# Expert items in pairs: one fp32r gather for two items, and the scatter in fp32r passes

## Chip, core and metric

The kernel runs on one core of one Trainium2 chip. The metric is the device time in microseconds. The kernel before was run three times: median 2162.56 us, from 2161.83 to 2163.13.

## What is computed

The program takes one sequence of 256 tokens with 1024 features through two blocks. The first has two attention layers, the second two layers of a convolution and delta-rule mixer, each followed by a feed-forward part: dense in the first layer, a mixture of experts in the second. The change lies in that last part and in the layer norm behind it. All numbers are fp32.

```
def moe_swiglu(x, router_w, w_gate, w_up, w_down):
    logits = (x @ router_w).astype(jnp.float32)
    top_v, top_i = lax.top_k(logits, TOP_K)
    gates = jax.nn.softmax(top_v, axis=-1)
    combine = jnp.sum(jax.nn.one_hot(top_i, N_EXPERTS) * gates[..., None], axis=-2)
    y = jnp.zeros_like(x)
    for e in range(N_EXPERTS):
        y = y + combine[..., e:e + 1] * swiglu(x, w_gate[e], w_up[e], w_down[e])
    return y
...
x = layer_norm_2(DEEPNORM_ALPHA * x + f, ln_ffn_g[layer], ln_ffn_b[layer])
```

TOP_K is 2, N_EXPERTS 8 and D_FF_EXPERT 3584, so one expert has 3 x 1024 x 3584 weights, 44 MB.

## The kernel before

**Items.** The 256 tokens lie in two tiles of 128. Each expert takes its tokens in a block of up to 128, an *item*; an expert with more tokens gets a second item (`list_items`, L2662). The engines loop over the items with a count read from memory (`Fori`), and the last item stands behind the loop. For each item the kernel gathers the columns of its tokens out of x by a matmul with a 0/1 matrix `pick` (`gather`, L1449), computes the two hidden products and the down product, and adds the result to `total` through a second matmul with the transposed, weighted matrix `pickT` (`scatter`, L1470).

**Precision.** A fp32 matmul is done by TensorE in several passes. The large products use fp32r operands in three passes: every operand is split into a rounded high part and a low part, and high x high, high x low and low x high are summed in PSUM (L1485 to L1487, L1502). Weights are split on the chip: ACT copies a piece into `his` (`split_hi`), DVE subtracts (`split_lo`, L2626). The gathered x is split in the same way (`gathered_hi`, `gathered_lo`, L2702), and so are the hidden values (`hidden_hi`, `hidden_lo`, L2714). The gather and the scatter themselves are plain fp32.

**Pieces and turns.** The weights of an item are 42 pieces of 1 MB (`piece_of`), which SP loads into 14 slots; `his` has three buffers. The work on the pieces goes in turns (`chunk(n, j)`, j from 0 to 6, and -2 and -1 ahead of the loop). A turn takes six pieces: four for one 512 wide part of gate and up (`up_pieces`), two for the down product of the part before (`down_pieces`). Between them stands `turn_hidden` (L1464), which transposes the hidden values into bank 4; ACT makes `he_hi` out of it, DVE `he_lo`, and `down_pieces` waits for `he_ready`. In turn 5 the order differs: its two down pieces come first, they end the item, and the four up pieces belong to the next item. So turn 5 is where the next gather stands:

```
if j == 5:
    turn_hidden(g - 1)
    ...
    gather(0)
    pe.wait_ge(S("he_ready"), g)
    gather(1)
    down_pieces(n, g - 1, s0)
```

`turn_picks` (L1457) transposes the weighted picks in turn 0. In turn 6 PE waits for `ye_copied` and scatters three quarters into banks 5, 0 and 1 and the last into bank 5 again; DVE adds them to `total` (`add_out`, L2722).

**Order on the engines.** Each engine works through its own list in order, and the orders are written out by hand: in every turn ACT does `split_hi` of its six pieces with the other steps tied to a place r between them, and DVE the same with `split_lo`. In turn 5 DVE does `hidden_lo` behind the second split (r = 1), in the other turns behind the fourth. ACT may split piece s only when PE has used piece s - 3. SP loads piece s + 14 when PE has used piece s.

**Start and end.** At the start PE computes the logits (L1549), DVE finds the two best experts, the places and the first picks (L2640 to L2656), PE gathers, and DVE does `combine` and `list_items`; only then does SP know which expert to load from piece 14 on. At the end come the last hidden values, two down pieces, the copy of ye, four scatters, four adds, the statistics and the norm of each tile, and one store of x. SP loads the norm's rows `lng` and `lnb` ahead of the stage.

## Time and profile before

| | us |
|---|---|
| median of 3 runs | 2162.56 |
| the profiled execution | 2165.7 |
| its span, first to last instruction | 2163.9 |
| expert stage, from the first piece's matmul (1145.61) to the end | 1018 |
| one item, steady | 125.2 |
| granted clock of TensorE, mean over the span | 0.973 |

Below, a row of the timeline gives the start in us from the span's start, the duration, the engine and the line; names of tiles stand without buffer numbers. In brackets stands how long the engine was idle before it and what it waited for. A fp32 matmul leaves two records. Matmuls are pipelined, so a record's duration is longer than the distance to the next. The granted clock is 1.00 at 2.4 GHz and 0.50 at 1.2 GHz.

### The profile page before, as it was taken

The numbers are of one execution on the slowest core, as the hardware profiler recorded it, in microseconds if no ns is written. First come the engines' busy times: TensorE is split into PE (matmuls) and PEld (weight loads), VectorE is DVE, ScalarE is ACT, GpSimd is POOL, SyncE is SP. The second block draws the span as 40 slices with busy tenths as digits, with TensorE's granted clock in tenths as the row PEclk, the third lists the DMA queues.
The fourth block names the chain that finished last, engine by engine and source line by source line (L and its number), as shares of the span: only waits on it lengthen the run. The fifth ranks groups of instructions, "written<-read, shape, count | busy, mean of one in ns | idle before, by whom it ended". The sixth has DMA issues, their size and how long they took to land.

```text
span 2163.9 us, 27922 instructions
## 1 busy us (share of the span) xinstructions
PE 2097.1 (97%) x10564; PEld 1664.2 (77%) x10564; DVE 1505.0 (70%) x1822; ACT 1004.5 (46%) x1074; POOL 51.2 (2%) x56
## 2 busy tenths in 40 slices
PE   7999999999998999999889999999999999999996
PEld 4786577766876799888748888888888888888885
DVE  4465434554597544449848988888888888888886
ACT  1121312022233343313236767766776776777674
POOL 0000000000011000001200000000000000000000
PEclk9998999999999999999989999999999999999998
DMA  9844042610621355453127999999998999999890
GB/s 356 282 141 151 30 156 88 225 60 24 218 74 40 117 191 180 175 179 115 41 108 295 395 349 370 347 349 367 329 375 323 373 347 349 347 350 376 322 348 20
DMA packets 238695, 502.20 MB, mean 232 GB/s; under 512 B 11259, under 2 KB 53011, under 8 KB 238611
## 3 DMA queue, kind: packets, MB, share of 16 engines
q1 hardware_dynamic: 238610, 501.03, 64.4%
q8 instruction: 58, 0.95, 0.2%
q14 instruction: 27, 0.21, 0.0%
HBM read 499.96 MB, written 1.05 MB: 232 GB/s over the span
## 4 chain that ended last, share of the span: by engine, by line
PE 89%; DVE 7%; ACT 2%; issue 1%; DMA 0%; SPq 0%; DVEq 0%; ACTq 0%
PE bank L1502 12%; PE bank L1485 9%; PE bank L1487 9%; PE bank L1486 9%; PE bank L756 6%; PE bank L1195 6%; PE bank L1063 3%; PE bank L988 3%; PE bank L764 3%; PE bank L1165 3%; PE bank L1432 2%; PE bank L1171 2%; PE bank L1403 2%; PE bank L1402 2%; PE bank L1401 2%; PE bank L1367 2%
## 5 line engine op out<-in xcount | busy, mean ns | idle before, releaser
L2626 DVE TENSOR_TENSOR ring_r<-ring,his 128x2048 fp32r<-128x2048 f32 x240 | 549.2, 2291 | 83.3 <-ACT his L1598 83.2
L1598 ACT ACTIVATE his<-ring 128x2048 fp32r<-128x2048 f32 x240 | 460.4, 1919 | 130.9 <-PE bank L1487 77.6
L1485 PE MATMUL bank<-his,xe_hi 128*128 128x512 f32 x896 | 356.0, 397 | 0.2 <-DVE ring_r L2626 0.2
L1487 PE MATMUL bank<-his,xe_lo 128*128 128x512 f32 x896 | 349.5, 390 | 0.0
L1486 PE MATMUL bank<-ring_r,xe_hi 128*128 128x512 f32 x704 | 274.0, 389 | 0.0
L2626 DVE TENSOR_TENSOR more_raw_r<-more_raw,his 128x2048 fp32r<-128x2048 f32 x96 | 219.8, 2291 | 32.1 <-ACT his L1598 32.0
L1598 ACT ACTIVATE his<-more_raw 128x2048 fp32r<-128x2048 f32 x96 | 184.2, 1919 | 57.4 <-PE bank L1502 31.9
L1485 PEld LDWEIGHTS bank<-his,xe_hi 128*128 128x128 f32 x896 | 168.3, 188 | 36.1 <-issue 1.7
L1487 PEld LDWEIGHTS bank<-his,xe_lo 128*128 128x128 f32 x896 | 168.2, 188 | 35.8
L1486 PEld LDWEIGHTS bank<-ring_r,xe_hi 128*128 128x128 f32 x704 | 132.3, 188 | 28.3 <-issue 1.7
L1195 PE MATMUL bank<-uT,ring 128*128 128x256 f32 (+1 forms) x768 | 149.2, 356 | 0.0
L756 PE MATMUL bank<-uT,ring 128*128 128x256 f32 (+4 forms) x688 | 145.6, 368 | 0.0
L1502 PE MATMUL bank<-his,he_hi 128*128 128x512 f32 x448 | 142.5, 399 | 1.9 <-DVE he_lo L2714 1.9
L1195 PEld LDWEIGHTS bank<-uT,ring 128*128 128x128 f32 x768 | 130.6, 198 | 15.3 <-issue 0.5
L1502 PE MATMUL bank<-his,he_lo 128*128 128x512 f32 x448 | 138.5, 390 | 0.0
L756 PEld LDWEIGHTS bank<-uT,ring 128*128 128x128 f32 (+3 forms) x688 | 114.4, 184 | 27.4 <-issue 6.5
L2450 DVE SCALAR_TENSOR_TENSOR cacc<-hpad,cvec,cacc 128x256 f32<-128x256 f32 x240 | 109.7, 530 | 0.1
L1401 PE MATMUL bank<-uT_r,ff_hi 128*128 128x256 f32 (+1 forms) x384 | 108.6, 283 | 0.0
L2124 DVE TENSOR_TENSOR ring_r<-ring,ff_hi 128x2048 fp32r<-128x2048 f32 (+1 forms) x34 | 74.2, 2226 | 49.4 <-ACT ff_hi L1598 49.4
L1402 PE MATMUL bank<-u_lo,ff_hi 128*128 128x256 f32 (+1 forms) x384 | 108.1, 282 | 0.0
L1403 PE MATMUL bank<-uT_r,ring_r 128*128 128x256 f32 (+1 forms) x384 | 108.1, 282 | 0.0
L1598 ACT ACTIVATE ff_hi<-ring 128x2048 fp32r<-128x2048 f32 (+1 forms) x34 | 61.4, 1858 | 85.1 <-PE bank L1403 57.0
(427 smaller groups left out, 3076.2 us busy)
## 6 DMA issues: line engine op xcount, KB each, us to landing
ring<-in_moe_w_gate_dram SPq DMA_DIRECT2D x96, 1024.0 KB, 5.2
ring<-in_moe_w_up_dram SPq DMA_DIRECT2D x80, 1024.0 KB, 5.3
ring<-in_moe_w_down_dram SPq DMA_DIRECT2D x64, 1024.0 KB, 4.9
more_raw<-in_moe_w_down_dram SPq DMA_DIRECT2D x48, 1024.0 KB, 5.0
ring<-in_w_in_dram SPq DMA_DIRECT2D x16, 2048.0 KB, 10.9
more_raw<-in_moe_w_up_dram SPq DMA_DIRECT2D x32, 1024.0 KB, 5.2
ring<-in_w_ada_dram SPq DMA_DIRECT2D x12, 2048.0 KB, 10.4
ring<-in_w_out_dram SPq DMA_DIRECT2D x8, 2048.0 KB, 8.4
```

Source lines behind the costliest of these rows:

```text
L756: last = mm(b[0:n, to + tokens.start:to + tokens.stop], w[:, k, a:a + n], uT[:, k, tokens], start=(k == 0), stop=(k == KD - 1))
L1195: last = mm(b[:, f * T + tokens.start:f * T + tokens.stop], w[:, k, a:a + P], uT[:, k, tokens], start=(k == 0), stop=(k == KD - 1))
L1401: mm(o, hi[:, k, a], u_hi[:, k, tokens], start=(k == 0), stop=False)
L1402: mm(o, hi[:, k, a], u_lo[:, k, tokens], start=False, stop=False)
L1403: last = mm(o, lo[:, k, a], u_hi[:, k, tokens], start=False, stop=(k == KD - 1))
L1485: mm(bank[b][:, :], xe_hi[:, k, :], hi[:, kk, :], start=(k == 0), stop=False)
L1486: mm(bank[b][:, :], xe_hi[:, k, :], lo[:, kk, :], start=False, stop=False)
L1487: last = mm(bank[b][:, :], xe_lo[:, k, :], hi[:, kk, :], start=False, stop=(k == KD - 1))
L1502: last = mm(bank[6 + c][:, :], a[:, k, :], w[:, kk, 512 * c:512 * c + 512], start=(q == 0 and k == 0 and a is he_hi and w is hi), stop=(q ...
L1598: return go(out, in_, ACT.Copy, scale=scale)
L2450: ins = stt(cacc[:, f, :], src, w, cacc[:, f, :], ALU.mult, ALU.add)
L2626: tt(piece_lo(s), piece_raw(s), piece_hi(s).bitcast(fp32), ALU.subtract).then_inc(S("lo_ready"), 1)
```

## The change

Items are worked on in pairs. The loop body holds two items (a = 0 and a = 1), and the last pair stands behind the loop.

- **Gather.** x is split once into `x_hi` and `x_lo` (`x_lo` in the place of x, `xe_lo` in the place of `lng` and `lnb`, `x_hi` and `ye_lo` over constants no longer needed). `pick` is 256 columns wide, and one gather serves both items: 16 fp32r matmuls of 256 columns with `x_hi`, 16 with `x_lo`. Each of the four parts f is copied by ACT (high) and by DVE (low, now a plain copy). The gather stands in turn 5 of the second item only, spread between the pieces: part 0 ahead of the down pieces, 1 and 2 behind each of them, 3 between the first two up pieces.
- **Even items.** In turn 5 of the first item of a pair, `turn_hidden` is followed by `down_pieces` directly.
- **Scatter.** The picks are no longer weighted; `turn_picks` collects the weights of the slots into one column (`gslot`) by two fp32 matmuls of one column. ye is scaled with it and split: ACT writes `ye_hi`, DVE `ye_lo` (`out_lo`), and a scatter is two fp32r matmuls.
- **Start.** DVE computes `total` and `x_lo`, ACT `x_hi`, ahead of the logits; `combine` comes behind the splits of turn -2, and `list_items` is somewhat longer.
- **End.** The last down product goes by column halves (`last_down`), so do the copies and scatters; `hidden_lo` comes ahead of the last split; adds and statistics alternate; `lng` and `lnb` are loaded behind the last up piece; x is stored in two halves.

The constants' order in memory changes as well, with no work of its own. The diff, cut to its core:

```diff
+        const, const2 = sb("const", [P, NCONST]), sb("const2", [P, NCONST2])
+        x = sb("x", [P, NT, D])
+        lng, lnb = sb("lng", [P, D]), sb("lnb", [P, D])
...
+        x_hi = sb("x_hi", [P, NT, D], fp32r)
+        ye_lo = sb("ye_lo", [P, D], fp32r)
+        sb("const2_kept", [P, NCONST + NCONST2 - KEPT_FIRST - (NT + 1) * D])
+        x_lo = sb("x_lo", [P, NT, D], fp32r)
+        xe_lo = sb("xe_lo", [P, 2, KD, P], fp32r)
...
-                elif s == 2 * RING:
-                    norm_rows(sp, NORMS - 1, A["ln_ffn_g_2"][1], A["ln_ffn_b_2"][1])
...
+            sp.wait_ge(S("piece_used"), more * (2 * NPIECE) + (NPIECE + chunk_at(4) + 4))
+            norm_rows(sp, NORMS - 1, A["ln_ffn_g_2"][1], A["ln_ffn_b_2"][1])
+            for i in range(NT):
+                sp.wait_ge(S("x_ready"), NT * (NORMS - 1) + i + 1)
+                sp.dma_start(out_dram[0, i * P:(i + 1) * P, :], x[:, i, :]).then_inc(S("stored"), 16)
+            sp.wait_ge(S("stored"), 16 * NT)
...
+            def gather(m, f, lo, b):
+
+                if f:
+                    pe.wait_ge(S("xe_lo_ready" if lo else "xe_hi_ready"), m * 4 + f)
+                src = x_lo if lo else x_hi
+                for kk in range(2):
+                    k = 2 * f + kk
                     for i in range(NT):
+                        last = mm(bank[b][:, kk * 2 * P:(kk + 1) * 2 * P], src[:, i, k * P:(k + 1) * P], pick[:, i, :],
+                                  start=(i == 0), stop=(i == NT - 1))
...
+            def turn_picks(a):
+
+                own = slice(a * P, (a + 1) * P)
+                for i in range(NT):
+                    nc.tensor.transpose(bank[5][:, i * P:(i + 1) * P], pick[:, i, own].bitcast(fp32), C("ident"))
+                for i in range(NT):
+                    last = mm(bank[5][:, NT * P:NT * P + 1], pick[:, i, own].bitcast(fp32), combc[:, i, a:a + 1],
+                              start=(i == 0), stop=(i == NT - 1))
...
+                mm(bank[b][:, :], pickT[:, at // 2, :], ye_hi[:, cs], start=True, stop=False)
+                mm(bank[b][:, :], pickT[:, at // 2, :], ye_lo[:, cs], start=False, stop=True).then_inc(S("scattered"), 1)
...
+            def first_up(n, a, m, s0, b):
 
                 for half in range(2):
+                    if half:
+                        gather_both(m, 3)
+                    pe.wait_ge(S("xe_hi_ready"), m * 4 + (2 * half + 2))
+                    pe.wait_ge(S("xe_lo_ready"), m * 4 + (2 * half + 2))
+                    up_piece(n, a, s0 + half, half, b)
+
+            def gather_both(m, f):
+
+                gather(m, f, False, 5)
+                gather(m, f, True, 4)
...
+            def last_down(n, g, s0):
+
+                pe.wait_ge(S("he_ready"), g + 1)
+                for c in range(2):
+                    for half in range(2):
+                        s = s0 + half
+                        if c == 0:
+                            pe.wait_ge(S("lo_ready"), n * NPIECE + (s + 1))
+                        hi, lo = piece_hi(s), piece_lo(s)
+                        for kk in range(2):
+                            k = 2 * half + kk
+                            for a, w in ((he_hi, hi), (he_hi, lo), (he_lo, hi)):
                                 last = mm(bank[6 + c][:, :], a[:, k, :], w[:, kk, 512 * c:512 * c + 512],
+                                          start=False, stop=(k == 3 and a is he_lo))
+                    last.then_inc(S("last_down"), 1)
...
+                to = a if j < 5 else 1 - a
                 if j == 0:
                     pe.wait_ge(S("acc_added"), n * 4 + 4)
                 if j == 5:
                     turn_hidden(g - 1)
+                if j == 5 and a == 1:
                     pe.wait_ge(S("picks_copied"), n + 1)
-                    pe.wait_ge(S("picked"), n + 2)
-                    gather(0)
+                    pe.wait_ge(S("picked"), m + 2)
+                    gather(m + 1, 0, False, 5)
                     pe.wait_ge(S("he_ready"), g)
-                    gather(1)
+                    gather(m + 1, 0, True, 4)
+                    down_piece(n, s0)
+                    gather_both(m + 1, 1)
+                    down_piece(n, s0 + 1)
+                    gather_both(m + 1, 2)
+                    first_up(n, to, m + 1, s0 + 2, b)
+                    s0 += 2
+                elif j == 5:
                     down_pieces(n, g - 1, s0)
                     s0 += 2
-                if j == 5:
-                    pe.wait_ge(S("xe_ready"), n * 2 + 4)
-                up_pieces(n, s0, b)
+                    up_pieces(n, to, s0, b)
+                else:
+                    up_pieces(n, to, s0, b)
                 if j > -2 and j != 5:
                     turn_hidden(g - 1)
                 if j == 0:
...
+                    pe.wait_ge(S("ye_split"), n * 2 + 2)
+                    for at, bk in enumerate((5, 0, 1)):
+                        scatter(n, at, bk)
...
+                for f in range(4):
+                    gather(0, f, False, 5 + 2 * (f % 2))
+                    gather(0, f, True, 4 + 2 * (f % 2))
...
+                act.wait_ge(S("x_ready"), NT * (NORMS - 2) + 1)
+                copy(x_hi[:, 0, :], x[:, 0, :]).then_inc(S("x_hi_ready"), 1)
                 copy_tile(("moe", 0), 1, 1)
                 act.wait_ge(S("x_ready"), NT * (NORMS - 1))
+                copy(x_hi[:, 1, :], x[:, 1, :]).then_inc(S("x_hi_ready"), 1)
...
+                def gathered_hi(m, f, b):
+
+                    act.wait_ge(S("gathered_hi"), m * 4 + (f + 1))
+                    copy(xe_hi[:, :, 2 * f:2 * f + 2, :], bank[b][:, :].rearrange("p (k a s) -> p a k s", k=2, a=2))\
+                        .then_inc(S("xe_hi_ready"), 1)
...
                         if j == 5 and r == 4:
                             copy_out(n)
+                        if j == 5 and a == 1 and r in (1, 2, 3, 4):
+                            gathered_hi(m + 1, r - 1, 5)
...
+                j = jobs["moe", 0, "xT11"]
+                filled(dve, j)
+                for i in range(NT):
+                    for c in range(2):
+                        cs = slice(512 * c, 512 * c + 512)
+                        ts(total[:, i, cs], x[:, i, cs], ALPHA, None, ALU.mult).then_inc(S("acc_added"), 1)
+                for i in range(NT):
+                    dve.wait_ge(S("x_hi_ready"), i + 1)
+                    dve.wait_ge(S("acc_added"), 2 * i + 2)
+                    tt(x_lo[:, i, :], x[:, i, :], x_hi[:, i, :].bitcast(fp32), ALU.subtract).then_inc(S("x_lo_ready"), 1)
...
+                def gathered_lo(m, f, b):
+
+                    dve.wait_ge(S("gathered_lo"), m * 4 + (f + 1))
+                    nc.vector.tensor_copy(xe_lo[:, :, 2 * f:2 * f + 2, :], bank[b][:, :].rearrange("p (k a s) -> p a k s", k=2, a=2))\
+                        .then_inc(S("xe_lo_ready"), 1)
...
+                def out_lo(n):
+
+                    dve.wait_ge(S("picks_copied"), n + 1)
+                    for c in range(2):
+                        cs = slice(512 * c, 512 * c + 512)
+                        dve.wait_ge(S("ye_hi_ready"), n * 2 + (c + 1))
+                        stt(ye_lo[:, cs], bank[6 + c][:, :], gslot[:, 0:1], ye_hi[:, cs].bitcast(fp32), ALU.mult, ALU.subtract)\
+                            .then_inc(S("ye_split"), 1)
...
+                        if j == 5 and a == 1 and r in (1, 2, 3, 4):
+                            gathered_lo(m + 1, r - 1, 4)
...
+                        if j == 5 and r == 5:
+                            out_lo(n)
...
+                for f in range(4):
+                    gathered_lo(0, f, 4 + 2 * (f % 2))
+                chunk(0, 0, -2)
                 combine()
-                gathered_lo(0, [1])
-                chunk(0, -2)
                 list_items()
-                chunk(0, -1)
+                chunk(0, 0, -1)
...
                 gated(n, g, 4)
+                hidden_lo(g)
                 split_lo(n, s + 1)
-                hidden_lo(g)
-                for at in range(4):
-                    add_out(n, at, at)
-                dve.wait_ge(S("acc_added"), n * 4 + 8)
+                out_lo(n)
                 for i in range(NT):
                     for c in range(2):
+                        add_out(n, 2 * i + c, 2 * i + c, turn=NT * c + i)
+                        dve.wait_ge(S("acc_added"), n * 4 + (4 + 2 * i + c + 1))
                         half_stats(i, c, total[:, i, :])
                     norm(NORMS - 1, i, total[:, i, :])
 

```

## Rows read from the trace of the kernel before

**Rows 1.** The page's first part: busy us, share of the span and instructions of each engine.

```profile
PE 2097.1 (97%) x10564; PEld 1664.2 (77%) x10564; DVE 1505.0 (70%) x1822; ACT 1004.5 (46%) x1074; POOL 51.2 (2%) x56
```

**Rows 2.** By window: us, PE, PEld, DVE, ACT, POOL busy; clock, DMA share, GB/s.

```profile
1160.00:2134.00 974.00, 973.49 (x4460) 799.59 (x4461) 847.26 (x513) 697.90 (x475) 0.00 (x0) 1.00 0.94 346
1160.00:1180.00 20.00, 20.00 (x92) 16.25 (x93) 18.99 (x14) 14.36 (x9) 0.00 (x0) 1.00 1.04 399
```

**Rows 3.** The timeline of turn 5, first and seventh item: start, us, what.

```profile
1257.96 2.28 DVE L2626 TENSOR_TENSOR more_raw_r<-more_raw,his 128x2048 fp32r<-128x2048 f32 x1
...
1258.44 0.60 PE L1467 MATMUL bank<-const,uT 128*128 128x128 f32 x4
...
1258.87 4.08 PE L1453 MATMUL bank<-pick,x 128*128 128x128 f32 x32
...
1259.08 0.60 ACT L1598 ACTIVATE he_hi<-bank 128x512 fp32r<-128x512 f32 x1 [1.24 <-PE bank L1467]
...
1260.16 0.68 DVE L2714 TENSOR_TENSOR he_lo<-bank,he_hi 128x512 fp32r<-128x512 f32 x1
...
1262.70 0.70 PE L1502 MATMUL bank<-his,he_hi 128*128 128x512 f32 x2
...
1265.73 1.93 ACT L1598 ACTIVATE his<-ring 128x2048 fp32r<-128x2048 f32 x1 [0.34 <-PE bank L1502]
...
1270.29 0.39 PE L1485 MATMUL bank<-his,xe_hi 128*128 128x512 f32 x1
...
1270.97 0.39 PE L1485 MATMUL bank<-his,xe_hi 128*128 128x512 f32 x1
...
2011.41 0.69 DVE L2714 TENSOR_TENSOR he_lo<-bank,he_hi 128x512 fp32r<-128x512 f32 x1
```

**Rows 4.** The timeline of PE in the dense stage.

```profile
799.93 0.28 PE L1401 MATMUL bank<-uT_r,ff_hi 128*128 128x256 f32 x1
...
802.09 0.28 PE L1401 MATMUL bank<-uT_r,ff_hi 128*128 128x256 f32 x1
```

**Rows 5.** The timeline of PE at the last item's last hidden values.

```profile
2134.92 0.60 PE L1467 MATMUL bank<-const,uT 128*128 128x128 f32 x4
2137.45 1.07 PE L1502 MATMUL bank<-his,he_hi 128*128 128x512 f32 x2 [1.94 <-DVE he_lo L2714]
```

**Rows 6.** The timeline of PE at three scatters of the first item.

```profile
1285.01 2.74 PE L1472 MATMUL bank<-ye,pickT 128*128 128x512 f32 x6
```

**Rows 7.** The timeline of PE at matmuls of one column.

```profile
601.31 2.85 PE L1268 MATMUL bank<-const,sq 128*128 128x1 f32 x25
```

**Rows 8.** The timeline of DVE and PE at the start of the expert stage.

```profile
1132.42 2.29 DVE L2626 TENSOR_TENSOR ring_r<-ring,his 128x2048 fp32r<-128x2048 f32 x1 [2.11 <-ACT his L1598]
...
1139.90 5.95 PE L1453 MATMUL bank<-pick,x 128*128 128x128 f32 x32 [1.20 <-DVE pick L2656]
...
1154.61 2.29 DVE L2626 TENSOR_TENSOR ring_r<-ring,his 128x2048 fp32r<-128x2048 f32 x1
...
1170.31 1.43 DVE L2755 TENSOR_SCALAR total<-x 128x512 f32<-128x512 f32 x4
```

**Rows 9.** One line's instructions on DVE: duration min/median/max in ns, first and last start.

```profile
L2392 DVE TENSOR_TENSOR mix<-mix,sg x4: 1218/1222/1225, 252.6 to 497.7; 128x1024 f32<-128x1024 f32 x4
```

**Rows 10.** The timeline of PE and DVE at the end.

```profile
2145.94 3.70 PE L1472 MATMUL bank<-ye,pickT 128*128 128x512 f32 x8 [1.17 <-ACT ye L1598]
...
2158.16 1.28 DVE L2087 SCALAR_TENSOR_TENSOR x<-x,lnmv,lnb 128x1024 f32<-128x1024 f32 x1
```

**Rows 11.** Busy time and granted clock by window, behind three waits of PE.

```profile
643.00:646.00 3.00, 3.00 (x4) 1.33 (x5) 3.00 (x9) 0.00 (x0) 0.00 (x0) 0.50 0.00 0
1041.00:1044.00 3.00, 3.00 (x20) 2.28 (x20) 2.94 (x8) 0.60 (x1) 0.68 (x1) 1.00 0.00 0
2138.00:2141.00 3.00, 3.00 (x9) 2.32 (x8) 0.00 (x0) 0.00 (x0) 0.00 (x0) 0.50 0.00 0
```

**Rows 12.** The waits of PE: us in total, times, longest us.

```profile
PE bank L1207 <- DVE vb L2544: 5.3, 2, 2.7
```

More of the change, by code:

```diff
@@ L136, in constants @@
     later["level0"] = lv[:, 0].T.copy()
+    later["tri_le"] = (row <= col).astype(np.float32)
+    later["tri_lt"] = (row < col).astype(np.float32)
+    later["iota"] = np.broadcast_to(r[None, :], (P, P)).astype(np.float32)
+    parts["fill"] = np.zeros((P, -sum(v.shape[1] for v in parts.values()) % 64), np.float32)
     at = {}
@@ new lines, in _ @@
+            with sp.Fori(0, more) as m:
+                e = [sp.value_load(items[0:1, bass.ds(m * 2 + (2 * NE + after), 1)], min_val=0, max_val=NE - 1) for after in range(3)]
+                for s in range(RAWS, RAWS + 2 * NPIECE):
+                    sp.wait_ge(S("piece_used"), m * (2 * NPIECE) + (s - RAWS + 1))
+                    load_piece(s, bass.ds(e[piece_of(s)[1]], 1))
+            e = [sp.value_load(items[0:1, bass.ds(more * 2 + (2 * NE + after), 1)], min_val=0, max_val=NE - 1) for after in range(2)]
@@ new lines, in down_pieces @@
+                down_piece(n, s0 + 1)
[5 more added lines that the diff above has]
+                        if c == 0:
+                            pe.wait_ge(S("lo_ready"), n * NPIECE + (s + 1))
+                        hi, lo = piece_hi(s), piece_lo(s)
+                        for kk in range(2):
+                            k = 2 * half + kk
+                            for a, w in ((he_hi, hi), (he_hi, lo), (he_lo, hi)):
@@ L1538, in chunk, with first_chunk @@
                     down_pieces(n, g - 1, s0 + 4)
+            def first_chunk():
+                for half in range(2):
+                    pe.wait_ge(S("xe_hi_ready"), 2 * half + 2)
+                    pe.wait_ge(S("xe_lo_ready"), 2 * half + 2)
+                    up_piece(0, 0, half, half, 0)
+                up_pieces(0, 0, 2, 1)
             def experts():
@@ L2696, in gathered_lo @@
-                def gathered_lo(m, halves=(0, 1)):
-                    for half in halves:
-                        dve.wait_ge(S("xe_hi_ready"), m * 2 + (half + 1))
-                        b = bank[5 - half][:, :].rearrange("p (f s) -> p f s", f=4)
-                        hi, lo = xe_hi[:, 4 * half:4 * half + 4, :], xe_lo[:, 4 * half:4 * half + 4, :]
-                        tt(lo, b, hi.bitcast(fp32), ALU.subtract).then_inc(S("xe_ready"), 1)
+                    ts(comb[:, :, 2 * NE:], chosen[:, :, 0:1], 0.0, None, ALU.mult)
```

248 lines of the change are left out of this document (113 added, 135 removed).

## Prediction

> **What bounds the kernel now.** I read the page's busy times first: TensorE (PE) is busy for 97% of the span, DVE for 70%, ACT for 46% [rows 1]. The change lies in the expert stage, so the window over that stage comes next [rows 2]: from 1160 to 2134 PE is busy for 973.49 of 974 us at the full clock, DVE for 847, ACT for 698. PE bounds it. The weights are no bound: the window from 1160 to 1180 moved 399 GB/s, the whole stage 346 GB/s. One item loads 42 pieces of 1.049 MB, which at 399 GB/s is 110 us, while an item takes 125.2 us (DVE's he_lo of turn 5 starts at 1260.16 in the first item and at 2011.41 in the seventh, six items later) [rows 2, 3]. But DVE has only 13% idle, and PE is fed through three buffers: a piece is copied by ACT (1.92 us), subtracted by DVE (2.29 us), then multiplied in 12 matmuls 227 ns apart, 2.72 us (the starts at 1270.29 and 1270.97 are three matmuls apart) [rows 3]. What counts is therefore PE's own work per item, plus every wait that the new order of the instructions opens on PE.
>
> **The gather.** Before, an item's gather is 32 records (16 fp32 matmuls of 128 columns). With what it waits for it fills PE from 1258.87 to 1262.70, 3.83 us [rows 3]. A pair's gather is 32 fp32r matmuls of 256 columns. The dense stage has the same form: 18 of them from 799.93 to 802.09, 120 ns each [rows 4], so 3.84 us for a pair in place of 7.66.
>
> But the old gather also covers a chain. Turn 5 begins with four transposes of the hidden values (1258.44); ACT then writes he_hi, and DVE writes he_lo, but only after the split of piece 1 that stands ahead of it in DVE's order (1257.96 to 1260.24). he_lo ends at 1260.84 and the down matmuls may begin [rows 3]. PE fills that time with the gather.
>
> *Even items (four of them, 0, 2, 4, 6)* have no gather now: turn_hidden is followed at once by down_pieces, which waits for he_ready. The trace has exactly this case once, at the end of the last item: transposes at 2134.92, down matmuls at 2137.45, 2.53 us later [rows 5]. Before, that distance in turn 5 is 1262.70 - 1258.44 = 4.26 us. So an even item gains 1.73 us, not 3.83: 4 x -1.73 = -6.9 us.
>
> *Odd items with a gather (1, 3, 5).* PE does the transposes (0.43) and 4 matmuls (0.48), then waits for he_ready until about 2.5 us after the transposes began: a gap of 1.6 us. Later first_up's second half needs the last copy of xe_lo. Follow the chain from the end of gather 2's high part: 0.25 us until ACT sees it, ACT copies (0.60, as he_hi), ACT splits piece 4 (1.92), DVE splits it (2.29), and only then DVE copies the last low part (0.69), with 0.1 for the hand-overs: 5.85 us. PE has meanwhile gather 2 low (0.48), one piece (2.72) and gather 3 (0.96): 4.16 us. A second gap of 1.7 us. Turn 5 is then 0.43 + 72 x 0.227 + 3.84 + 1.6 + 1.7 = 23.9 us, against 20.7 before (0.43 + 3.83 + 16.4) [rows 3]: 3 x +3.2 = +9.6 us. The gathers of the loop together come to +2.7 us, where bare matmul time would give -15.3.
>
> **Scatter.** An fp32 matmul of 512 columns is two records. Six records last 2.74 us, each 0.59 and overlapping, so (2.74 - 0.59) / 5 = 0.43 us apart [rows 6]; four scatters take 8 x 0.43 = 3.44 us. Now 8 fp32r matmuls of 227 ns, 1.82 us: 7 x -1.62 = -11.3 us; the last item's is in the end. The split of ye moves to DVE (two operations of 0.69) ahead of turn 6's first split: ready at about 1279.13 where PE asks at 1279.13, so nothing. DVE's four adds cost 2.8 us in turn 6 against PE's 1.8 of scatter; by the rows' distances DVE then still comes 0.5 to 0.7 us before PE. I take 0, at most 0.5 per item (3.5 in all).
>
> **turn_picks.** The transposes stay; two fp32 matmuls of one column come, 4 records. The nearest row: 25 records of one column in 2.85 us, 114 ns each [rows 7]. 8 x 0.46 = +3.7 us. The Trainium skill (TensorE: Matmul & The Clock Gate, "Wait — 56ns, not 53.3ns?") says that start to start never falls under about 25 ns however few the columns; by that floor the term would be 0.8. The row carries a weight load with each matmul, as here, and it decides. The extra copy of gslot on ACT and the longer pick_tokens on DVE lie under PE.
>
> **The start.** DVE gets, ahead of the logits, four products of total (1.43 us; their old place cost PE nothing) and two subtractions of 128x1024 (1.22 us each in the nearest row) [rows 8, 9], and ACT two copies. The second x_lo ends at about 1133.6, the logits follow, and split_lo(0,0), which began at 1132.42, begins at 1134.1: +1.7 us. Two more picks: +0.5. The gather, at the low clock, was 5.95 us from 1139.90 on. The new one streams as many columns, but each part waits for the copy of the part before it; with the clock rising at the same distance I get 6.7. Piece 0 starts 3.0 us later. Then combine stands behind the splits of pieces 2 and 3 and list_items has some 0.8 us more: DVE's split of piece 4, which ended at 1156.90, ends at about 1162.1, PE waiting 2.6 us. Together +5.2 us. The loads of pieces 14 and on begin that much later too, with 20 us in hand. Between 3 and 8.
>
> **The end.** he_lo goes ahead of the last split, so the down matmuls begin 0.5 us sooner; the column halves hide half of the ye copies. The last scatter ends near 2146.6, where it ended at 2149.6 [rows 10]. DVE then mixes adds and statistics and finishes the last x at 2157.5, where it was 2159.4; and the last store is half as long: 0.9 us. -2.9 us, between -1.5 and -4. lng and lnb are loaded some 15 us ahead of their use.
>
> **Sum without the clock:** 2.7 - 11.3 + 3.7 + 5.2 - 2.9 = -2.6 us.
>
> **The clock.** After the wait at the end of the last item the granted clock is 0.50 (1.2 GHz) from 2138 to 2141 [rows 11]: three us do the work of 1.5, and with the ends of the stretch I count 1.7 us lost. The new gaps follow work as dense as that. But no gap of this size is sure to do it: line L1207 waits 2.7 us for vb once in each of the two mixers, and the first wait is followed by 0.50 (643 to 646), the second by 1.00 (1041 to 1044) [rows 11, 12]. So two gaps of three are followed by the low clock, and the new ones are mostly shorter than these: ten new gaps in the loop of 1.6 to 2.1 us and one of 2.6 at the start, a fall behind half or a little less; I take 5, +8.5 us (0 to 18.7).
>
> **Forecast:** +5.9 us. The profiled execution took 2165.7 us (span 2163.9), 3.1 over the median of 2162.56. On its scale 2171.6, on the median's 2168.5.
>
> **The rivals.**
> - *The gaps come, the clock stays up:* -2.6 us, 2160.0, no difference or nearly. For it: one gap of three left the clock alone, and the new ones are shorter than it. Against: the one gap behind turn_hidden in this very stage did not.
> - *The gaps don't come* (faster). It decides at he_ready and xe_lo_ready: if he_lo were written before the split of piece 1, or ACT and DVE ran a piece ahead, PE would find both ready. Then 4 x -3.83 for the even items, 0 for the odd: -15.3 - 11.3 + 3.7 + 5.2 - 2.9 = -20.6, 2142.0. For it: he_hi is ready by 1259.68, so only DVE's order makes the wait, and gather 1 is well spread. Against: all seven turns 5 have he_lo at the same place (a period of 125.2 us from the first to the last in [rows 3]), and DVE's order there is unchanged.
> - *More is lost:* every gap costs 1.7 us (+18.7): 2178.7. Or DVE, with 0.7 us more per item behind the scatter than PE gives it time for, stops PE in turn 0 as well: up to 3.5 us more.
> - *The pairs don't come out even:* an odd number of items would add an empty one, a whole item of 125 us. The period of 125.2 us goes seven times into the stage behind the first turn, so there are eight items and four full pairs; I give it nothing.
>
> **Chances.** Gaps with about half the falls 0.5 (2163 to 2174); gaps without falls 0.2; no gaps 0.12; more lost 0.15; 0.03 for anything else. A difference under 0.2% (4.3 us) a measurement can hardly tell. Slower by more: most of the first and all of the fourth, 0.55. Within: all but a little of the second, the low edge of the first, 0.27. Faster: 0.18. The range leaves out the case without gaps and the far end of the fourth: 2154 to 2178.
>
> **What would show it.** In turn 5 of even items, PE's waits for he_lo of about 2.0 us, four of them; in odd items one of 1.6 for he_lo and one of 1.7 for xe_lo; windows with a clock of 0.50 behind some; a scatter of 1.8 us; piece 4 of the first item about 5 us later; the last x at about 10 us after the last scatter. If PE's waits on DVE in the loop come to under 5 us instead of the 18 here, the step on he_ready is wrong and the kernel is faster. If they are there and no window of the loop has a clock under 1, the result is 2160.

## The result and the profile after

The changed kernel takes 2183.29 us (median of 4 runs, 2179.99 to 2188.47) where the kernel before takes 2162.36 (4 runs): a ratio of 1.0094, interval 1.0079 to 1.0109. It is 20.9 us slower; 5.9 were forecast. Every ratio below is to the kernel before, run beside it, with its 95% interval in brackets. The profiled execution took 2184.97 us with a span of 2183.2, 19.3 over the span of before.

The first part of the page answers to [rows 1]: TensorE (PE) is busy 7 us less, in a longer span. Below it the row of the queue that brings in instructions, which had 58 packets and 0.95 MB before.

```profile
PE 2089.9 (96%) x10468; PEld 1652.1 (76%) x10468; DVE 1514.0 (69%) x1841; ACT 1008.1 (46%) x1084; POOL 51.4 (2%) x56
...
q8 instruction: 90, 1.47, 0.3%
```

The waits of PE from 1150 us to the end, in us in total, times, longest. The kernel before has three there: 1.9 for he_lo, 1.2 for ye and 0.2 at piece 4.

```profile
PE bank L1532 <- DVE he_lo L2811: 7.6, 4, 1.9
PE bank L1501 <- issue: 5.7, 2, 3.1
PE bank L1499 <- DVE xe_lo L2798: 4.3, 3, 1.4
PE bank L1466 <- DVE he_lo L2811: 4.1, 3, 1.4
PE bank L1499 <- issue: 2.5, 2, 1.3
PE bank L1499 <- DVE ring_r L2722: 2.0, 1, 2.0
PE bank L1555 <- DVE he_lo L2811: 1.5, 1, 1.5
PE bank L1490 <- DVE ye_lo L2820: 0.6, 1, 0.6
PE bank L1555 <- DVE more_raw_r L2722: 0.5, 1, 0.5
```

The waits on DVE are those of the prediction. Not foreseen are the four called *issue*: PE's matmuls are late with nothing to wait for. The timeline shows them (start, us, what), together with turn 5 of an even item (1261.84, 1264.35), the scatter (1286.98), the two gaps of an odd item's turn 5 (1388.40, 1401.65), turn_picks' matmuls of one column (1439.50) and the end, which answers to [rows 3, 5, 6, 10].

```profile
1145.34 0.40 PE L1499 MATMUL bank<-his,xe_hi 128*128 128x512 f32 x1
...
1158.62 0.50 PE L1499 MATMUL bank<-his,xe_hi 128*128 128x512 f32 x1 [2.00 <-DVE ring_r L2722]
...
1261.84 0.60 PE L1484 MATMUL bank<-const,uT 128*128 128x128 f32 x4
1264.35 0.72 PE L1532 MATMUL bank<-his,he_hi 128*128 128x512 f32 x2 [1.91 <-DVE he_lo L2811]
...
1286.98 0.48 PE L1490 MATMUL bank<-ye_hi,pickT 128*128 128x512 f32 x1
...
1290.54 0.40 PE L1499 MATMUL bank<-his,xe_hi 128*128 128x512 f32 x1
...
1293.32 0.40 PE L1499 MATMUL bank<-his,xe_hi 128*128 128x512 f32 x1
...
1388.40 0.73 PE L1466 MATMUL bank<-pick,x_lo 128*128 128x256 f32 x4 [1.36 <-DVE he_lo L2811]
...
1401.65 0.49 PE L1499 MATMUL bank<-his,xe_hi 128*128 128x512 f32 x1 [1.43 <-DVE xe_lo L2798]
...
1430.37 0.49 PE L1499 MATMUL bank<-his,xe_hi 128*128 128x512 f32 x1 [1.18 <-issue]
...
1435.73 0.50 PE L1501 MATMUL bank<-his,xe_lo 128*128 128x512 f32 x1 [2.55 <-issue]
...
1439.50 0.51 PE L1476 MATMUL bank<-combc,pick 128*128 128x1 f32 x4
1439.86 0.47 PE L1499 MATMUL bank<-his,xe_hi 128*128 128x512 f32 x1
...
2159.89 0.49 PE L1555 MATMUL bank<-his,he_hi 128*128 128x512 f32 x1 [1.49 <-DVE he_lo L2811]
...
2167.97 0.50 PE L1490 MATMUL bank<-ye_hi,pickT 128*128 128x512 f32 x1 [0.64 <-DVE ye_lo L2820]
...
2178.80 1.28 DVE L2173 SCALAR_TENSOR_TENSOR x<-x,lnmv,lnb 128x1024 f32<-128x1024 f32 x1
```

1430.37 is the first matmul of the loop's second pass. The third pass begins with the same pair of stalls (1.30 and 3.13): 8.2 us in all, behind the loop's two jumps back. The kernel before jumps back six times and has none: its waits of PE over the same stretch name no *issue*.

The second thing not foreseen is in the distance of ordinary matmuls. From 1290.54 to 1293.32 lie 12 fp32r matmuls of 512 columns, 232 ns apart, where before it was 227 [rows 3]. Over the whole stage, three up matmuls take 0.6951 us on the mean (before 0.6817) and six down matmuls 1.3771 (before 1.3611). With 896 and 224 such groups that is 12.0 + 3.6 = 15.6 us.

The granted clock falls in two places of the loop only. By window: us, busy PE, PEld, DVE, ACT, POOL, clock, DMA share, GB/s.

```profile
1522.00:1525.00 3.00, 3.00 (x10) 2.34 (x10) 2.29 (x1) 0.28 (x1) 0.00 (x0) 0.64 0.72 277
1525.00:1528.00 3.00, 3.00 (x12) 2.40 (x11) 0.00 (x0) 1.67 (x1) 0.00 (x0) 0.79 0.23 23
...
1696.00:1699.00 3.00, 3.00 (x10) 2.40 (x9) 1.07 (x1) 1.90 (x1) 0.00 (x0) 0.66 0.55 153
```

The first follows a wait for he_lo, the second the issue stall of 3.13 us. The first costs 3 x 0.36 + 3 x 0.21 = 1.7 us, as a fall did in the prediction. The kernel before has a fall of its own, behind the wait of 1.94 us in the last item [rows 5, 11]; after, with 1.49 us there, has none: its clock is 1.00 from 2156 to 2165.

### The profile page after: what moved, and what is told of

Its sections match the earlier page's. It is cut to its first block, busy times and chain, and to the rows that moved or that the text cites. A ratio compares the mean times of both kernels' runs of the same rounds, so it can differ in the third digit from the quotient of the medians.

```text
span 2183.2 us, 27738 instructions
## 1 busy us (share of the span) xinstructions
PE 2089.9 (96%) x10468; PEld 1652.1 (76%) x10468; DVE 1514.0 (69%) x1841; ACT 1008.1 (46%) x1084; POOL 51.4 (2%) x56
## 4 chain that ended last, share of the span: by engine, by line
PE 88%; DVE 7%; issue 2%; ACT 2%; DMA 0%; SPq 0%; DVEq 0%; ACTq 0%
PE bank L1532 12%; PE bank L1501 9%; PE bank L1499 9%; PE bank L1500 9%; PE bank L765 6%; PE bank L1204 6%; PE bank L997 3%; PE bank L1072 3%; PE bank L773 3%; PE bank L1174 3%; PE bank L1441 3%; PE bank L1180 2%; PE bank L1410 2%; PE bank L1411 2%; PE bank L1412 2%
## 5 line engine op out<-in xcount | busy, mean ns | idle before, releaser
L1501 PE MATMUL bank<-his,xe_lo 128*128 128x512 f32 x896 | 355.1, 396 | 5.7 <-issue 5.7
L1532 PE MATMUL bank<-his,he_hi 128*128 128x512 f32 x440 | 136.8, 392 | 7.6 <-DVE he_lo L2811 7.6
L1532 PEld LDWEIGHTS bank<-his,he_hi 128*128 128x128 f32 x440 | 82.4, 189 | 26.2 <-DVE more_raw_r L2722 8.6
```

What stands on the lines that cost most here:

```text
L1501: last = mm(bank[b][:, :], xe_lo[:, a, k, :], hi[:, kk, :], start=False, stop=(k == KD - 1))
L1532: last = mm(bank[6 + c][:, :], a[:, k, :], w[:, kk, 512 * c:512 * c + 512], start=(q == 0 and k == 0 and a is he_hi and w is hi), stop=(q ...
```

## The experiments

Three theories had to be told apart. **Places:** the new buffers moved where the operands begin in SBUF, and that sets the matmuls' distance. **Layout:** the paired xe_hi and xe_lo (two items side by side) set it. **Loop:** the issue stalls come from the jump back to a longer body; the rival is that they come from the pairs' order of work. The table gives where each operand begins, as the remainder by 256 bytes of its start address in a partition (the *residue*; from the program's layout), and what the traces gave. *Streamed* operands are the pieces of the weights (his, ring_r, more_raw_r), *loaded* ones the stationary xe_hi, xe_lo and he. *Three up* is the distance from one high x high matmul to the next, three matmuls later; *six down* the same for the down product.

| kernel | ring_r | more_raw_r, his | xe_hi, he | xe_lo | three up, us | six down, us |
|---|---|---|---|---|---|---|
| before | 128 | 128 | 128 | 128 | 0.6817 | 1.3611 |
| after | 128 | 160 | 160 | 128 | 0.6951 | 1.3771 |
| e1 | 128 | 192 | 192 | 128 | 0.6965 | 1.3827 |
| e2 | 128 | 160 | 160 | 160 | 0.6916 | 1.3768 |
| e3 | 128 | 192 | 192 | 192 | 0.6877 | 1.3776 |
| e5 | 128 | 0 | 0 | 128 | 0.6933 | 1.3757 |
| e8 | 128 | 128 | 160 | 160 | 0.7001 | 1.3999 |
| e12 | 128 | 0 | 0 | 0 | 0.6911 | 1.3751 |
| e9 | 128 | 128 | 128 | 128 | 0.6820 | 1.3627 |
| e10 | 128 | 128 | 128 | 128 | 0.6818 | 1.3628 |
| e15 | 192 | 192 | 192 | 192 | 0.6819 | 1.3607 |

### Four first looks: e1 to e4

**e1**, the kernel after with everything behind `items` 32 bytes on:

```
         items = sb("items", [P, 4 * NE + 1], mybir.dt.int32)
+        sb("shift", [P, 8])
```

> The changed kernel with 32 unused bytes ahead of the staged tiles, so that his, more_raw, xe_hi and he_hi start on a multiple of 64 bytes again, as in the kernel before (in the changed kernel the longer constants moved them to an odd multiple of 32). Theory A, the start address sets the distance between the up matmuls: three of them take 0.681 us again instead of 0.695, 896 x 0.0136 = 12 us less than the changed kernel, some 2171. Rival B, the distance comes from the new shape or place of xe_hi and xe_lo, or from the longer loop: still 0.695 and no change, some 2183.

2184.38 us (4 runs), three up 0.6965: no gain. That a multiple of 64 is enough is refuted.

**e2**, the kernel before with the same line.

> The kernel before with the same 32 bytes, so that its staged tiles start on an odd multiple of 32 bytes. Theory A: three up matmuls take 0.695 us and the kernel is 12 us slower, some 2174.5. Rival B: 0.681 us and 2162.4, since neither shape nor place nor loop changed.

2176.3 us (4 runs), ratio 1.0060 (1.0042 to 1.0078), three up 0.6916, six down 1.3768. The kernel before, with not one instruction changed, lost 13 us by a shift of 32 bytes. Places matter by themselves.

**e3**, the kernel before with 32 bytes behind the constants and 32 ahead of the staged tiles, which moves x as the change does.

> The kernel before with 32 unused bytes behind the first constants and 32 ahead of the staged tiles: const2, x and the norm's rows move to a multiple of 64, the staged tiles stay on one. In the changed kernel the time up to the second tile's transposes ahead of the experts is 3.9 us shorter than before. Theory A: that comes from the address of x and const2, so the kernel is some 3.9 us faster, 2158.5, with those transposes near 1124. Rival: it is a matter of when the low clock falls and differs from run to run: 2162.4.

2168.93 us (10 runs), ratio 1.0024 (1.0015 to 1.0034), three up 0.6877. It is slower, not 3.9 us faster. Its one profiled execution, the fastest of the ten, does have the transposes early, at 1120.53, but so has that of e8 (1120.11), whose x kept its place. So the rival holds: that time differs between profiled executions, and nothing of it can be put down to the place of x.

The stage alone is free of that. From the first up matmul to the end of the span it takes 1018.3 us in before and in e15, 1024.7 in e3, 1027.3 in e12, 1028.2 in e2 and 1039.2 in e8: the order of the distances in the table. (Before and e15 each hold one clock fall under work, 1.7 us, in it, the other four none.)

**e4**, the kernel after with PE's loop over the pairs written out (the number of pairs fixed, as these inputs give it):

```
-                more = pe.value_load(...)
-                with pe.Fori(0, more) as m:
+                more = 3
+                for m in range(more):
                     for a in range(2):
```

> The changed kernel with TensorE's loop over the pairs written out three times (the number of pairs behind the loop is taken as three, as these inputs have it). In the changed kernel TensorE stands 1.2 and 2.6 us behind its first jump back and 1.3 and 3.1 behind its second, waiting for nothing that the profile names. Theory C, the jump back to a body twice as long costs them: the four gaps go, 8.2 us and a fall of the clock less, some 2173 to 2175. Rival D, the gaps come from something else at that place (loads of instructions as such): they stay, or others come all along the longer code, and the time stays near 2183 or rises.

2169.89 us (10 runs), 13.4 less than after. The stalls at the loop's start are gone. The trace still lists three of 1.29 under *issue* (1400.42, 1653.28, 1906.18): these are the three gaps for xe_lo, which carry another name there, since the 1.43 for xe_lo have gone from its list. So 8.2 us of stalls were taken away, the other gaps are 0.8 us shorter in all, and e4's profile has none of after's two clock falls (3.4 us). That is 12.4 us, where the medians differ by 13.4 and the two profiled spans by 14.4; the rest has no row.

### Multiples of 128, and the parts by themselves: e5 to e8

**e5**, the kernel after with 96 bytes ahead of the expert stage's staged tiles alone:

```
         place[0] = raws
+        sb("shift_raw", [P, 24])
...
         place[0] = fourth
+        sb("shift", [P, 24])
```

> The kernel after, with 96 bytes per partition put ahead of the expert stage's staged tiles alone, so that more_raw, his, xe_hi and he_hi begin at multiples of 128 bytes again as in the kernel before (xe_lo, at a multiple of 128 already, and x stay where they are). Theory A' (the matmuls' distance follows from where the tiles begin within 128 bytes; 32 and 64 bytes behind such a multiple both cost): three up matmuls back from 0.695 us to 0.682, six down matmuls from 1.377 to 1.361, and with 896 and 224 of them 12.0 + 3.6 = 15.6 us less, so about 2168. Rival B (the distance is a matter of the paired layout of xe_hi and xe_lo, 256 columns of two items, or of the rest of the changed program): 0.695 and 2183 as they were. Rival C (any move helps or harms by a couple of us): up triple between 0.685 and 0.69.

2180.37 us (5 runs), 0.6933 and 1.3757. 2168 was expected by the theory that a multiple of 128 is enough (A'). It falls, and the layout theory stands for the moment.

**e6**, the same with the loop written out.

> The same with TensorE's loop over the pairs written out three times, for the number of pairs that these inputs give. If the issue stalls come from the jump back and the distance from the places, the two add up: 13.4 us less for the loop as in the run that wrote it out alone, 15.6 less for the places: about 2183.3 - 29 = 2154, which would be below the kernel before (2162.4). If A' falls, about 2169 as the written-out kernel took before.

2169.01 us (8 runs), the case where A' falls.

**e7**, the kernel before with the scatter of the change alone:

```
-                mm(bank[b][:, :], pickT[:, at // 2, :], ye[:, ...], start=True, stop=True)
+                mm(bank[b][:, :], pickT[:, at // 2, :], ye_hi[:, cs], start=True, stop=False)
+                mm(bank[b][:, :], pickT[:, at // 2, :], ye_lo[:, cs], start=False, stop=True)
```

with turn_picks on unweighted picks, the weight as the copy's scale, and DVE's ye_lo as in the change.

> The kernel before with one part of the change alone: the scatter in two fp32r passes, with unweighted picks and the weight of each place as the scale of the copy. Per-item gather, the loop over items, the places of all staged tiles and the end over all columns stay. By the terms of the sum: seven items' scatters 7 x -1.62 = -11.3, turn_picks' two one-column matmuls 8 x 0.46 = +3.7, and at the end two more splits of 1.2 us ahead of the scatter and four shorter ones, about +0.5: 2162.4 - 7.1 = 2155.3. Rival: what TensorE gains is lost again in weaker cover (no gain, 2162), or the clock falls more often.

2153.64 us (6 runs), ratio 0.9958 (0.9942 to 0.9974): 8.5 us faster, 7.1 expected. Its staged tiles lie where they lay before, and the distance is 0.6823.

**e8**, the kernel before with 32 bytes between `his` and `xe_hi`.

> The kernel before with 32 bytes put between his and xe_hi: the moving operands (more_raw, his, ring) stay at multiples of 128 bytes, only the stationary ones (xe_hi, xe_lo, he_hi, he_lo) and what lies behind them move by 32. If the moving operand's place sets the distance: up triple 0.682, down six 1.361, time 2162.4. If the stationary one's does: 0.69 and 1.377, about 2176 as with all of them moved.

2182.97 us (5 runs), ratio 1.0098: the slowest distance of all. The timeline of PE; 12 matmuls take 2.80 us:

```profile
1201.58 0.40 PE L1486 MATMUL bank<-his,xe_hi 128*128 128x512 f32 x1
...
1204.38 0.40 PE L1486 MATMUL bank<-his,xe_hi 128*128 128x512 f32 x1
```

Here the streamed operands kept their place and only the loaded ones moved. It is neither kind by itself: compared with e2, where both moved by 32 bytes, it is worse. That points to how the two stand to each other.

The traces of e2, e3 and e12 show it within one kernel. There his, more_raw_r, xe_hi, xe_lo and he all agree, and only ring_r differs. A low piece lies either in more_raw_r or in ring_r. Three up matmuls with more_raw_r take 0.682 (e2), 0.683 (e3) and 0.684 us (e12), as in before; with ring_r they take 0.694, 0.689 and 0.693. In before both take 0.682 to 0.683, in e8 both 0.700. From e2's timeline, 12 matmuls with ring_r (2.77 us) and 12 with more_raw_r (2.72 us):

```profile
1283.79 0.39 PE L1486 MATMUL bank<-his,xe_hi 128*128 128x512 f32 x1
1284.02 0.40 PE L1487 MATMUL bank<-ring_r,xe_hi 128*128 128x512 f32 x1
...
1286.56 0.39 PE L1486 MATMUL bank<-his,xe_hi 128*128 128x512 f32 x1
...
1303.64 0.39 PE L1486 MATMUL bank<-his,xe_hi 128*128 128x512 f32 x1
1303.86 0.39 PE L1487 MATMUL bank<-more_raw_r,xe_hi 128*128 128x512 f32 x1
...
1306.36 0.39 PE L1486 MATMUL bank<-his,xe_hi 128*128 128x512 f32 x1
```

### The same residue of 256: e9 to e12, e15

**e9** and **e10** put 224 and 480 bytes where e5 put 96; e10 also has the loop written out.

> The kernel after with 224 bytes put ahead of the expert stage's staged tiles: more_raw, his, xe_hi and he_hi then begin 128 bytes behind a multiple of 256, as ring_r and xe_lo do and as all of them did in the kernel before. Theory A'' (what counts is that the operands, both the streamed and the loaded ones, begin at the same residue of 256 bytes): up triple 0.682 us, down six 1.361, 15.6 us less than 2183, about 2168. Rival B (the paired layout of xe_hi and xe_lo or the rest of the program sets the distance): 0.693 to 0.695, about 2181. The issue stalls behind the jump back stay either way.

> The kernel after with TensorE's loop over the pairs written out and 480 bytes put ahead of the staged tiles, so that each of them begins at the same residue of 512 bytes as in the kernel before. A'': 0.682 and 1.361 and 2169 - 15 = 2154. If 512 bytes are the period and not 256, only this one of the two gets 0.682. Rival B: 0.693 and 2169 for both.

e9 took 2174.15 us (7 runs, 2167.28 to 2177.3; the profiled span is 2168.0), e10 2160.77 (11 runs), ratio 0.9984 (0.9972 to 0.9996). Both have the distance of before (0.6820 and 0.6818), with the paired layout as it is. The layout theory falls. In e9's timeline 12 matmuls take 2.73 us:

```profile
1288.26 0.39 PE L1501 MATMUL bank<-his,xe_hi 128*128 128x512 f32 x1
...
1290.99 0.39 PE L1501 MATMUL bank<-his,xe_hi 128*128 128x512 f32 x1
```

Since 128 and 384 by 512 do equally well, the period is 256 bytes and not 512. e9 gained 9 us on the median (11 by the two ratios) where 15.6 were expected; on the profiled spans it is 15.2, 1.7 of them one clock fall less. Its distance is shown, its whole gain in time is not: the runs scatter over 10 us, and only one of them has a trace. e10 came out 6.8 us above the expectation; its profile has two clock falls, 3.4 us, and the other half has no row.

**e12**, the kernel before with 128 bytes ahead of the staged tiles.

> The kernel before with 128 bytes put ahead of the staged tiles: more_raw, his, xe_hi, xe_lo and he begin at multiples of 256 bytes, ring_r stays 128 bytes behind one. If multiples of 128 are enough (theory A', with the paired layout to blame for the rest): 0.682 and 1.361, 2162. If the operands need the same residue of 256 (A''): up triple about 0.69, six about 1.376, 2162 + 10 = 2172.

2172.39 us (11 runs, 2163.96 to 2177.29), ratio 1.0035 (1.0022 to 1.0048), three up 0.6911: as the theory of 256 bytes has it. That the median meets the expected 2172 to half a us is luck, with runs that far apart.

**e15**, the kernel before with 64 bytes ahead of everything, ring_r too.

> The kernel before with 64 bytes put ahead of everything, ring_r too, so that ring_r, more_raw_r, his, xe_hi, xe_lo and he all begin 192 bytes behind a multiple of 256 (128 in the kernel before). If only their agreement counts: up triple 0.682, six 1.361, 2162.4. If the residue 128 itself is what is fast (every fast layout so far had it): up triple 0.688 to 0.70, six about 1.377, 2170 or more.

2164.29 us (10 runs), ratio 1.0004 (0.9991 to 1.0017), 0.6819 and 1.3607. So no residue is special; the operands have to agree.

**e11**, e7 with the end of the change (last down pieces by column halves, adds and statistics by halves, a store for each tile).

> The kernel before with two parts of the change: the scatter in fp32r passes (2153.6 alone) and the end by column halves (the last down pieces by halves, last hidden_lo ahead of the last split, adds and statistics by halves, each x tile stored for itself). The term of the sum was -2.9, 0.5 of it the earlier hidden_lo: about 2150.7. Rival: the end gains nothing without the pairs, 2153.6.

2152.47 us (5 runs), ratio 0.9941 (0.9922 to 0.9960), faster than both kernels. From the first up matmul to the end of the span e11 takes 1008.8 us (2150.7 - 1141.91), e7 1010.8 (2151.7 - 1140.92): neither has a clock fall in the loop or at the wait for he_lo, and the end is worth 2.0 of the 2.9 us.

### The body's length, and the gap ahead of he_lo: e13, e14

**e13**, the kernel before with two items in one body of PE's loop.

```
-                with pe.Fori(0, more) as n:
-                    for j in range(NQ):
-                        chunk(n, j)
-                n = more
+                with pe.Fori(0, 3) as m:
+                    for a in range(2):
+                        for j in range(NQ):
+                            chunk(m * 2 + a, j)
+                for j in range(NQ):
+                    chunk(6, j)
+                n = 7
```

> The kernel before with TensorE's loop alone changed: one body holds two items (three passes, the seventh item written out behind it, the counts fixed for these inputs), so its body has 1108 matmuls instead of 554, as many as the kernel after has. The work, its order and all waits stay. If a jump back to a body of this length is what stalls TensorE: two jumps, each with issue stalls of 3.4 to 4.4 us within the first 6 us behind it, 2 x 3.9 = +7.8, about 2171. Rival (the stalls come from the pairs' own order of work or from its waits at the start of the body): no stall, 2163.

2166.84 us (11 runs), ratio 1.0019 (1.0010 to 1.0028). The page's row of the instruction queue, and PE's timeline behind the two jumps:

```profile
q8 instruction: 91, 1.49, 0.3%
```

```profile
1425.83 0.49 PE L1485 MATMUL bank<-his,xe_hi 128*128 128x512 f32 x1 [0.84 <-issue]
...
1429.45 0.50 PE L1486 MATMUL bank<-more_raw_r,xe_hi 128*128 128x512 f32 x1 [0.39 <-issue]
...
1678.52 0.49 PE L1485 MATMUL bank<-his,xe_hi 128*128 128x512 f32 x1 [1.26 <-issue]
...
1684.06 0.79 PE L1486 MATMUL bank<-more_raw_r,xe_hi 128*128 128x512 f32 x1 [2.30 <-issue]
```

The same work in the same order, and the stalls of the pairs are there: 4.8 us of them, with +3.9 us on the median, where 7.8 were expected. The body's length makes them, and their size varies (1.2 and 3.6 us a jump here, 3.7 and 4.4 in after). The profile has one clock fall as well, at the stall of 2.30 us.

The instruction queue goes from 58 packets to 91, as in after (90). e4, which has code of its own for every pass and no jump, needs 83. So after brings in its body anew for each pass, and seven packets more, while before, with seven passes, stays at 58.

The Trainium skill (Runtime: NRT & Kernel Launch, "Instruction fetch mechanics") says that PE holds 2048 instructions, refilled in blocks of 256, and that a taken branch to a target outside the current window of two pages has to fetch it first. The number 2048 agrees with the runs on both sides. Between two jumps the trace of before records 574 matmuls (554, of which the fp32 ones leave two records each), 574 weight loads and 56 others, about 1200, and it loops without a stall; after has about 2360 (1124 matmuls) and e13 about 2400 (1148), and both stall. A window of two blocks, 512 instructions, doesn't agree: a body of 1200 would be outside it. Where between 1200 and 2360 the stall begins no run here shows.

**e14**, e10 with he_lo made ahead of the second split of turn 5:

```
                     for r in ...:
+                        if j == 5 and r == 1:
+                            hidden_lo(g - 1)
                         split_lo(n, s0 + r)
```

> The kernel of e10 with VectorE's order changed in turn 5: he_lo is made ahead of the split of the second down piece instead of behind it. In the trace of after he_hi is there at 1263.08 and the split ends at 1263.61, so he_lo starts 0.5 us earlier, in all seven items: waits of TensorE for he_lo 7.4 down to 5.4 (4 times) and 4.2 down to 2.7 (3 times), 2160.8 - 3.5 = 2157.3. Rival: the split that comes later then holds up the second down piece by as much, no gain.

2154.28 us (6 runs), ratio 0.9961 (0.9947 to 0.9975), 6.5 less than e10 (5.0 by the two ratios; 6.3 on the profiled spans). The waits of PE:

```profile
PE bank L1534 <- DVE he_lo L2813: 5.6, 4, 1.4
...
PE bank L1468 <- DVE he_lo L2813: 2.8, 3, 0.9
```

They fell from 7.4 and 4.2 us: 3.2 of the 3.5 expected. On the spans the other 3 us are the two clock falls of e10's profile (0.91 in the windows 1260 to 1280 and 1760 to 1780), of which e14's has none; whether e14's other runs have fewer falls is not shown. DVE's order made 0.5 us of each gap; 1.4 us (even items) and 0.9 us (odd) remain and are the chain of transposes, ACT and DVE itself.

## Why the prediction was off

The direction was right, slower; the size was not (5.9 forecast, 20.9 measured). And the direction came by luck: the sum without the clock was -2.6, only the clock term made it slower, and that term was too high, while the two costs that did make the kernel slower had no term at all. Its sum against the trace, in its own steps:

- **Even items' turn 5:** 2.53 us from transposes to down matmuls forecast, 2.51 measured (1261.84 to 1264.35), four times. Right.
- **Odd items' turn 5:** gaps of 1.6 and 1.7 forecast, 1.36 and 1.43 measured, three times each. Right, 1.5 us too dear in all. e14 confirms the named cause, DVE's order.
- **Scatter and turn_picks:** -11.3 + 3.7 forecast. The scatter's matmuls are of the kind and distance of all others, and the four matmuls of one column take 0.36 us (1439.50 to 1439.86), 90 ns each, where I took 114 from another place; that is 8 x 0.1 = 0.8 us too dear. e7 alone gained 8.5 us (interval 5.6 to 12.5), against 7.6. Right.
- **Start:** +5.2 forecast. The first piece began 1145.34 - 1124.05 = 21.3 us behind the transposes of the second x tile, before 1145.61 - 1127.91 = 17.7: +3.6 for 3.0. PE's wait at piece 4 is 2.00 for 2.6. Right. That these transposes came 3.9 us sooner on the clock is not the change's: the start of the first up matmul lies between 1137.77 (e3) and 1148.06 (e2) in kernels that are alike up to there.
- **End:** -2.9 forecast. From the first of the last down matmuls to the end of the span 23.3 us (2183.2 - 2159.89) where it was 26.4 (2163.9 - 2137.45), and the wait ahead of them 1.49 for 1.94: -3.6. But 1.7 of it is the clock fall that before has there and after has not, so the end itself gave -1.9, as in e11 (-2.0). About 1 us too good, within its range of -1.5 to -4.
- **The clock**, "a fall behind half or a little less; I take 5, +8.5 us": the first step that failed. A fall costs 1.7 us as said, but they are rare. After has two in its loop, one of them behind a gap that I had named. Over the eight profiled kernels with these gaps (after, e1, e4, e5, e6, e9, e10, e14) the falls are 2, 2, 0, 1, 0, 1, 2 and 0. Two of the eight stand behind issue stalls of 3 us (after, e1), the other six all behind the even items' gap of 1.9 us, of which seven of the kernels have 28: one in five. None stands behind the gaps of 0.9 to 1.5 us, of which there are more. The prediction priced all ten alike, from three gaps of 1.9 to 2.7 us. The nearest of the three, the wait for he_lo at the last item of before, was itself the rarer case: of the eight profiles that have it at 1.8 to 1.9 us (before, e2, e3, e7, e8, e12, e13, e15) only those of before and e15 have a fall behind it. This term was about 5 us too high.
- **What the sum had no term for**, the step that made the miss: the cost of the changed parts was counted and everything around them taken as it was. Two things were not. First, two items in one loop body doubled PE's code, and the jump back then stalls: 8.2 us in the trace; e4 has it gone, and e13 shows it in the kernel before. I counted the jumps nowhere. Second, "12 matmuls 227 ns apart", read from before, was taken over for the pieces after ("72 x 0.227"), as if it could not change. But the first constants are ten columns longer, 2240 for 2230, which moves the staged tiles by 32 bytes, and xe_lo lies elsewhere, at residue 128: 15.6 us over the stage. e9 and e10 get the distance of before back by places alone.

On the spans: 5.9 forecast, less 5.0 for the clock, less 1.5 and 0.8 for the gaps and the one-column matmuls, plus 8.2 and 15.6, less the 3.9 that came ahead of the change's first step: 18.5. The end's -3.6 for -2.9, the fall of before included, makes it 17.8 of the measured 19.3; 1.5 us have no row.

Take both unforeseen costs away and the forecast's own part remains. e10 stands at 2160.8 with its ratio 0.9984, a difference of -3.5 us (-6.1 to -0.9), where the sum without the clock was -2.6 and the forecast with it +5.9. And the paired gather is then seen for what it is: e10 has it and e11 does not, and e10 is 8.3 us slower (2160.77 against 2152.47); the prediction's terms for the gathers and the start are 2.7 + 5.2 = 7.9. (e10's profile has two clock falls, e11's none, so up to 3.4 us of it may be the clock's.) The paired gather loses its cover in the even items and opens two gaps in the odd ones, which eat the 15 us of matmul time that it saves.

**What stays open.** Why operands at unlike residues slow PE: the runs show that it is so for the pair of streamed and loaded operands (e8), not which unit makes the two wait for each other. The distances within one kernel differ by pair of instructions, from 227 to 235 ns, and I found no rule that gives each. Where between 1200 and 2360 instructions the stall begins was not tried. About 1 of e4's 13.4 us has no row, nor has the part of the gain that is missing on the medians of e9 and e10.

**The rivals.** That the gaps don't come is refuted: PE's waits on DVE in the loop are 7.6 + 4.3 + 4.1 = 16.0 us. That more is lost behind the scatter is too: PE has no wait in turn 0. The rival without falls (2160.0) was nearer to the change's own part than the forecast; e10, though with two falls in its profile, took 2160.8.

## What to carry to other kernels

When an edit adds or resizes a buffer, compare the start addresses of every matmul operand before and after, by 256 bytes: here 32 bytes cost more than any part of the change saved, and padding gives the distance back for nothing. Before putting two iterations into one loop body, count the engine's instructions in it, weight loads included, and look for *issue* waits behind the jump back. And a piece of work that is made shorter may have been the cover of a chain beside it (here the gather over he_hi and he_lo): only the part beyond the chain's length is gained.

## What the runs showed of the hardware

- fp32r matmuls of 512 columns stand 227 ns apart when the streamed and the loaded operands begin at the same residue of 256 bytes (four layouts), and 229 to 233 ns when they don't (seven). Of the seven, four are the kernel before with padding and no other change, 5 to 21 us slower. Where only ring_r differs (e2, e3, e12), only the up matmuls of pieces in ring_r stand further apart.
- A jump back on PE costs 1.2 to 4.4 us with a body of some 2400 instructions, in two stalls 3 to 6 us apart, and nothing that the trace shows with 1200.
- A gap of 1.8 to 1.9 us in dense work was followed by the lower clock in 6 of 28 cases in the loop and in 2 of 8 at the last item, one of 0.9 to 1.5 us in none of some 50, an issue stall of 2.3 to 3.1 us in 3 of 7 (after, e1, e13); a fall cost 1.7 us.
